# Input stage of a two-layer decoder: turning tokens, high and low parts and the first weight slots

## The reference

```python
def rms_norm(x, w):
    x32 = x.astype(jnp.float32)
    y = x32 * lax.rsqrt(jnp.mean(x32 * x32, axis=-1, keepdims=True) + NORM_EPS)
    return (y * w.astype(jnp.float32)).astype(x.dtype)

def swiglu(x, w_gate, w_up, w_down):
    return (jax.nn.silu(x @ w_gate) * (x @ w_up)) @ w_down
```

## Time and profile before

| | us |
|---|---|
| median of 3 runs | 2236.66 |
| lowest and highest | 2235.32 to 2239.92 |
| profiled execution, device time | 2238.05 |
| its span in the profile | 2236.3 |
| TensorE busy in it | 2173.0 (97%) |
| VectorE busy | 1013.6 (45%) |
| ScalarE busy | 760.5 (34%) |

### The profile page before, as it was taken

The page is one execution under the profiler, slowest core; times in us unless marked ns, Lnnn a source line. Parts: engine busy times, 40 slices in busy tenths (PEclk is TensorE's granted clock), DMA queues, the critical chain, the costliest instruction groups (busy, mean ns, idle before and its releaser), DMA issues.

```text
span 2236.3 us, 38348 instructions
## 1 busy us (share of the span) xinstructions
PE 2173.0 (97%) x16050; PEld 2050.6 (92%) x16050; DVE 1013.6 (45%) x1385; ACT 760.5 (34%) x1232; POOL 111.1 (5%) x105
## 2 busy tenths in 40 slices
PE   6999999999989899999999999999999999999998
PEld 5999999998989889999999999999998788888887
DVE  5544422666475364444216444421663346444423
ACT  3322222335433443222224322222352454222222
POOL 2000000100032100000000000000000010000000
PEclk9999999999899999999999999999999999999999
DMA  3333332321110113323321333332232122333232
GB/s 100 104 93 87 98 117 81 74 77 43 44 39 1 46 50 104 94 85 104 104 84 48 103 94 92 97 104 75 64 86 67 47 58 84 94 94 94 93 113 76
DMA packets 328447, 179.69 MB, mean 80 GB/s; under 512 B 15834, under 2 KB 323329, under 8 KB 328351
## 3 DMA queue, kind: packets, MB, share of 16 engines
q1 hardware_dynamic: 326992, 175.30, 27.0%
q0 software_dynamic: 1024, 2.86, 0.5%
q10 hardware_dynamic: 334, 0.14, 0.0%
HBM read 176.16 MB, written 2.12 MB: 80 GB/s over the span
## 4 chain that ended last, share of the span: by engine, by line
PE 93%; DVE 3%; ACT 2%; DMA 1%; issue 1%; POOL 0%; ACTq 0%; DVEq 0%; POOLq 0%
PE psum L591 67%; PE psum L603 10%; PE psum L791 5%; PE psum L2226 1%; DVE w_hl L514 1%; PE psum L1781 1%; PE psum L2243 1%; PE psum L2693 0%; PE psum L1756 0%; PE psum L657 0%; DMA rows_vec<-dn_norm_w 0%; PE psum L2709 0%; PE psum L2704 0%; DMA stage<-even_w_in 0%; PE psum L1741 0%
## 5 line engine op out<-in xcount | busy, mean ns | idle before, releaser
L591 PE MATMUL psum<-x_hl,w_hl 128*128 128x264 f32 (+1 forms) x9120 | 1242.9, 299 | 9.3 <-DVE w_hl L514 3.8
L591 PEld LDWEIGHTS psum<-x_hl,w_hl 128*128 128x128 f32 x9120 | 1187.4, 190 | 60.7 <-issue 12.1
L514 DVE TENSOR_TENSOR w_hl<-stage,w_hl 128x1024 fp32r<-128x1024 f32 (+1 forms) x310 | 396.0, 1277 | 366.3 <-ACT w_hl L507 366.2
L507 ACT ACTIVATE w_hl<-stage 128x1024 fp32r<-128x1024 f32 (+1 forms) x310 | 339.8, 1097 | 234.3 <-PE psum L591 92.1
L591 PE MATMUL psum<-acts,w_hl 128*128 128x264 f32 x2376 | 288.9, 284 | 0.0
L591 PEld LDWEIGHTS psum<-acts,w_hl 128*128 128x128 f32 x2376 | 288.6, 188 | 0.0
L1332 DVE TENSOR_TENSOR t_both<-psum,rinv 128x528 f32<-128x528 f32 (+1 forms) x88 | 61.9, 703 | 303.4 <-PE psum L591 303.4
L1134 ACT ACTIVATE acts<-t_both 128x528 f32 (+3 forms) x88 | 56.6, 643 | 399.5 <-DVE t_both L1335 399.5
L603 PE MATMUL psum<-x_hl,w_hl 128*128 128x264 f32 (+1 forms) x1344 | 175.6, 290 | 6.8 <-DVE w_hl L514 4.6
L603 PEld LDWEIGHTS psum<-x_hl,w_hl 128*128 128x128 f32 x1344 | 169.6, 193 | 10.1 <-DVE w_hl L514 5.0
L1326 DVE TENSOR_TENSOR t_both<-psum,rinv 128x528 f32<-128x528 f32 (+1 forms) x88 | 61.9, 703 | 182.6 <-PE psum L591 182.5
(11 more groups left out here) (325 smaller groups left out, 1322.2 us busy)
## 6 DMA issues: line engine op xcount, KB each, us to landing
stage<-ffn_w_gate SPq DMA_DIRECT2D x88, 512.0 KB, 3.8
stage<-ffn_w_up SPq DMA_DIRECT2D x88, 512.0 KB, 3.8
stage<-ffn_w_down SPq DMA_DIRECT2D x48, 704.0 KB, 4.7
stage<-odd_w_in SPq DMA_DIRECT2D x24, 512.0 KB, 3.9
stage<-ffn_w_down SPq DMA_DIRECT2D x22, 512.0 KB, 3.4
stage<-even_w_in SPq DMA_DIRECT2D x18, 512.0 KB, 4.2
stage<-even_w_out SPq DMA_DIRECT2D x8, 512.0 KB, 3.7
stage<-odd_w_out SPq DMA_DIRECT2D x8, 512.0 KB, 3.6
```

The costliest lines, as they stand in the source:

```text
L507: act.activation(weights(core.w_hl[:, slot.ring, 0, :], *kind), weights(core.stage[:, slot.stage, :], *kind), ACT.Copy).then_inc(core.w_hi, 1)
L514: dve.tensor_tensor(weights(core.w_hl[:, slot.ring, 1, :], *kind), weights(core.stage[:, slot.stage, :], *kind), weights(core.w_hl[:, slot ...
L591: op = pe.matmul(out, lhs, moving[:, moved, kt, t0:t0 + n], start=first and part + moved == 0, stop=last and part == 1)
```

## The change

The tokens load as two transfers, features 0 to 511 first, the others behind the first slot's weights. TensorE waits only for identity and norm weights, turns these, then turns k-tiles 0 and 1 and from then on runs products of the first two slots between the turns: slot 0's k-tile two before the turned one behind each turn from the third on, and two k-tiles of slot 1 behind each of the last three turns. The other constants come after the last turn. Two double banks take turns for the turned k-tiles. ScalarE makes the high parts straight from PSUM, a left side of 272 tokens and a right side of 256, while VectorE copies the other side into `h`; then VectorE makes the low part, ScalarE the square into a buffer of its own for each k-tile. The weight splits of slots 0, 1 and 2 stand at k-tiles 0, 3 and 5. After all eight, VectorE adds the squares of four, two and one k-tiles in three additions in place of GpSimd's eight operations. The token sum moves two k-tiles ahead of the end of slot 2. The core of the diff (left out: constants of the counting in `Norm.count`, semaphores, unused ones removed):

```diff
 ROW_BANKS = (5, 7, 4, 6)
+INPUT_SIDES = ((0, META + 2 * P, 0), (META + 2 * P, 2 * P, 1))
+INPUT_SLOTS = 2
...
+        self.in_squares = self.at("in_squares", [P, DT, TOK], self.arena + 4 * FT * TOK)
...
 def sync_program(core, sp, a):
-    sp.dma_start(core.rows_x, a["x"][0].rearrange("(b p) d -> p b d", p=P)).then_inc(core.tok_in, 16)
+    load_tokens(core, sp, a, 0)
     sp.dma_start(core.rows_meta[:, :], a["meta_tokens"]).then_inc(core.tok_in, 16)
...
+def load_tokens(core, sp, a, half):
+    cols = slice(half * D // 2, (half + 1) * D // 2)
+    sp.dma_start(core.rows_x[:, :, cols], a["x"][0].rearrange("(b p) d -> p b d", p=P)[:, :, cols])\
+        .then_inc(core.tok_right if half else core.tok_in, 16)
+
+
 def load_slot(core, sp, a, phase, i, u):
     slot = Slot(phase, i, u)
+    if phase is core.phases[0] and slot.peeled and slot.local == 1:
+        load_tokens(core, sp, a, 1)
     if not slot.peeled or slot.count() > 2:
         sp.wait_ge(core.w_lo, slot.count(2))
...
+def input_bank(kt):
+
+    return 4 + 2 * (kt % 2)
+
+
+def tensor_input(core, pe, phase):
+
+
+    k = core
+    slots = [Slot(phase, 0, u) for u in range(INPUT_SLOTS)]
+
+    def turn(kt):
+        if kt >= 2:
+            pe.wait_ge(k.x_hi, kt - 1)
+            pe.wait_ge(k.h_new, 2 * (kt - 1))
+        if kt == 0:
+            pe.wait_ge(k.tok_in, 32)
+        elif kt == DT // 2:
+            pe.wait_ge(k.tok_right, 16)
+        cols = slice(kt * P, (kt + 1) * P)
+        bank = input_bank(kt)
+        pe.transpose(k.psum[:, bank, 0:META], k.rows_meta[0:META, cols], k.ident[0:META, 0:META])
+        for b in range(NBLK):
+            at = META + b * P if b < 2 else (b - 2) * P
+            op = pe.transpose(k.psum[:, bank + b // 2, at:at + P], k.rows_x[:, b, cols], k.ident[:])
+        op.then_inc(k.tok_flip, 1)
+
+    def run(slot, kt):
+        if kt == 0:
+            pe.wait_ge(k.w_lo, slot.count())
+        pe.wait_ge(k.x_lo, kt + 1)
+        slot.out_pair = slot.pair
+        op = products(k, pe, phase, slot, kt, kt, k.x_hl, kt == 0, kt == DT - 1)
+        if kt == DT - 1:
+            op.then_inc(k.slot_used, 1)
+
+    turn(0)
+    turn(1)
+    pe.wait_ge(k.cols_ready, 1)
+    for kt in range(2, DT // 2 + 1):
+        turn(kt)
+        run(slots[0], kt - 2)
+    for kt in range(DT // 2 + 1, DT):
+        turn(kt)
+        run(slots[0], kt - 2)
+        run(slots[1], 2 * (kt - DT // 2 - 1))
+        run(slots[1], 2 * (kt - DT // 2 - 1) + 1)
+    pe.wait_ge(k.x_hi, DT)
+    pe.wait_ge(k.h_new, 2 * DT)
+    pe.wait_ge(k.consts_set, 5)
+    pe.wait_ge(k.consts_in, 16 * (CONST_LOADS - SCALAR_LOADS))
+    pe.wait_ge(k.vectors_in, 16 * (SCALAR_LOADS - 2))
+    pe.transpose(k.psum[:, 7, 2 * P:2 * P + VEC_ROWS], k.rows_vec[0:VEC_ROWS, :], k.ident[0:VEC_ROWS, 0:VEC_ROWS])
+    pe.matmul(k.psum[0:QH, 6, 0:512], k.table[:], k.bucket_hot[:, 0:512], start=True, stop=True)
+    pe.matmul(k.psum[0:QH, 7, 0:V_ALL - 512], k.table[:], k.bucket_hot[:, 512:V_ALL], start=True,
+              stop=True).then_inc(k.cols_flip, 1)
+    for slot in slots:
+        run(slot, DT - 2)
+        run(slot, DT - 1)
+
...
+        tensor_input(k, pe, phase)
+    elif not whole_first:
         tensor_first(k, pe, phase)
+    done = INPUT_SLOTS if begins else RING - 1 if whole_first else RING
     for slot in group:
         weights_ready(slot)
...
-                token_sum(k, pe, phase.before)
             op = products(k, pe, phase, slot, kt, kt, k.x_hl, kt == 0, kt == DT - 1)
             if kt == DT - 1:
                 op.then_inc(k.slot_used, 1)
 
     def step(i, u):
-        if isinstance(i, int) and i == 0 and (u < RING - 1 or not whole_first):
+        if isinstance(i, int) and i == 0 and u < done:
             return
         slot = Slot(phase, i, u)
         slot.out_pair = slot.pair
@@ -902,8 +980,9 @@
         weights_ready(slot)
         if turned:
             pass
-        elif phase.kind != "out" and isinstance(i, int) and i == 0:
-            pe.wait_ge(k.root_ready, 1)
+        elif begins and isinstance(i, int) and i == 0:
+            if u == RING - 1:
+                pe.wait_ge(k.root_ready, 1)
         elif phase.kind == "out" and slot.local == RING - 1:
             pe.wait_ge(k.even.o_full, NBLK + 1)
         elif not (isinstance(i, int) and i == 0):
@@ -917,6 +996,8 @@
             else:
                 pe.wait_ge(k.scaled, i * RING + (u + phase.evac0 - RING + 1))
         for kt in range(DT):
+            if begins and isinstance(i, int) and i == 0 and u == INPUT_SLOTS and kt == DT - 2:
+                token_sum(k, pe, phase.before)
...
 def token_sum(core, pe, norm):
 
-    pe.wait_ge(core.sq_added, DT)
+    pe.wait_ge(core.sq_added, 3)
+    pe.wait_ge(core.cols_ready, 4)
...
 def tensor_program(core, pe):
     k = core
-    pe.wait_ge(k.consts_set, 5)
-
-    pe.wait_ge(k.vectors_in, 16 * SCALAR_LOADS)
-    pe.wait_ge(k.consts_in, 16 * (CONST_LOADS - SCALAR_LOADS))
...
-    for kt in range(DT):
-        pair = (kt + 2) % RING
-        if kt >= 2:
-            pe.wait_ge(k.h_new, max(kt - RING + 1, 1))
-            pe.wait_ge(k.cols_ready, 4)
-        pe.transpose(k.psum[:, 2 * pair, 0:META], k.rows_meta[0:META, kt * P:(kt + 1) * P], k.ident[0:META, 0:META])
-        for b in range(NBLK):
-            at = META + b * P if b < 2 else (b - 2) * P
-            op = pe.transpose(k.psum[:, 2 * pair + b // 2, at:at + P], k.rows_x[:, b, kt * P:(kt + 1) * P], k.ident[:])
-        op.then_inc(k.tok_flip, 1)
-    pe.wait_ge(k.h_new, DT)
+    pe.wait_ge(k.norms_in, 32)
+    pe.transpose(k.psum[:, 0, 0:12 * DT], k.rows_norm[0:12 * DT, :], k.ident[0:12 * DT, 0:12 * DT])\
+      .then_inc(k.cols_flip, 1)
     for kind, step in k.steps:
         if kind == "dense":
             tensor_dense(k, pe, step)
...
+def scalar_input(core, act):
+
+
+    k = core
+    first = k.phases[0]
+    act.wait_ge(k.cols_flip, 1)
+    act.activation(k.norm_cols[:, :], k.psum[:, 0, 0:12 * DT], ACT.Copy).then_inc(k.cols_ready, 1)
+    act.wait_ge(k.cols_ready, 1)
+
+    def square(kt):
+        act.wait_ge(k.h_new, 2 * kt + 2)
+        act.activation(k.in_squares[:, kt, :], k.h[:, kt, :], ACT.Square).then_inc(k.sq_made, 1)
+
+    for kt in range(DT):
+        col = first.before.pre_col + kt
+        for side, (t0, n, bank) in enumerate(INPUT_SIDES):
+            if side == 0:
+                act.wait_ge(k.tok_flip, kt + 1)
+            else:
+                act.wait_ge(k.h_new, 2 * kt + 1)
+            act.activation(k.x_hl[:, 0, kt, t0:t0 + n], k.psum[:, input_bank(kt) + bank, 0:n], ACT.Copy,
+                           scale=k.norm_cols[:, col:col + 1]).then_inc(k.x_hi if side else k.in_high, 1)
+        if kt:
+            square(kt - 1)
+        if kt in INPUT_SPLITS:
+            split_hi(k, act, Slot(first, 0, INPUT_SPLITS.index(kt)), (DT, P))
+    square(DT - 1)
+    act.wait_ge(k.cols_flip, 2)
+    act.activation(k.vec_cols[:, 0:VEC_ROWS], k.psum[:, 7, 2 * P:2 * P + VEC_ROWS], ACT.Copy).then_inc(k.cols_ready, 1)
+    act.activation(k.bias_row[0:QH, 0:512], k.psum[0:QH, 6, 0:512], ACT.Copy).then_inc(k.cols_ready, 1)
+    act.activation(k.bias_row[0:QH, 512:V_ALL], k.psum[0:QH, 7, 0:V_ALL - 512], ACT.Copy).then_inc(k.cols_ready, 1)
+
+
 def scalar_norm(core, act, norm):
     k = core
     if norm.split:
         scalar_split(k, act, norm)
         return
     load_table(k, act, ACT.Sqrt)
-    for kt in range(DT):
-        act.wait_ge(k.h_new, norm.h0 + kt + 1)
-        tile = k.h[:, kt, norm.t0:TOK]
-        col = norm.pre_col + kt
-        act.activation(k.x_hl[:, 0, kt, norm.t0:TOK], tile, ACT.Copy,
-                       scale=k.norm_cols[:, col:col + 1]).then_inc(k.x_hi, 1)
-        if kt >= 2:
-            act.wait_ge(k.sq_added, kt - 1)
-        buf = k.t_up if kt % 2 else k.t_gate
-        act.activation(buf[:, norm.t0:TOK], tile, ACT.Square).then_inc(k.sq_made, 1)
-        if kt == DT // 2:
-            split_ahead(k, act, split_hi, norm.next, 0, 0)
+    split_ahead(k, act, split_hi, norm.next, 0, 0)
     root(k, act, norm)
     load_table(k, act, ACT.Silu)
+    act.wait_ge(k.bias_stored, 16)
 
 
...
 def scalar_program(core, act, a):
     k = core
-    for dst, src in const_rows(k, a)[0:SCALAR_LOADS]:
+    for dst, src in const_rows(k, a)[0:2]:
+        act.dma_start(dst, src).then_inc(k.norms_in, 16)
+    for dst, src in const_rows(k, a)[2:SCALAR_LOADS]:
         act.dma_start(dst, src).then_inc(k.vectors_in, 16)
-    split_hi(k, act, Slot(k.phases[0], 0, 0), (DT, P))
-    act.wait_ge(k.cols_flip, 1)
-    act.activation(k.norm_cols[:, :], k.psum[:, 0, 0:12 * DT], ACT.Copy).then_inc(k.cols_ready, 1)
-    act.activation(k.vec_cols[:, 0:VEC_ROWS], k.psum[:, 1, 0:VEC_ROWS], ACT.Copy).then_inc(k.cols_ready, 1)
-    act.activation(k.bias_row[0:QH, 0:512], k.psum[0:QH, 2, 0:512], ACT.Copy).then_inc(k.cols_ready, 1)
-    act.activation(k.bias_row[0:QH, 512:V_ALL], k.psum[0:QH, 3, 0:V_ALL - 512], ACT.Copy).then_inc(k.cols_ready, 1)
-    act.wait_ge(k.consts_set, 5)
```

(78 more changed lines are left out.)

6 lines of the change are left out of this document (removed).

## The result

The changed kernel takes **2224.03 us** (median of 5, 2222.86 to 2225.03) against 2236.66: ratio 0.9941, 95% interval 0.9929 to 0.9953. The profiled execution took 2223.76, its span 2222.0.

A forecast was written before the change was run, and what follows sets the result against it. TensorE is busy for 97% of the span, so only the start, before products run, can pay. The fourth slot starts at 42.9 instead of 50.26, a gain of 7.4 us: 2236.66 becomes 2229.3, range 2226 to 2234.5.

The forecast's parts named there:

- The rise of TensorE's clock: At the start, among turns and products: TensorE stays at the low level until 26.3 us, then runs at the high one.
- the fourth slot: End of the start: the fourth weight slot's products begin at 42.9 us instead of 50.26, a gain of 7.4 us.
- everything after it should move with it: Behind the fourth slot's start: all later work shifts by the same time, so that start alone judges the change.
- an uncertainty of 1 or 2: Whole time: the shown runs lie 4.6 us apart, which adds 1 or 2 us of uncertainty to the range.
- no new gap: Sign to look for: TensorE shows no new gap behind the fourth slot.
- The rule weighed: Turns among products: transposes don't raise the clock, so they would hold it down and the gain would be gone.
- rivals 1 and 3: Clock stays low through last turn and constants (2237.0, milder 2234.0; chance 0.14 together), or through slot 2 (2243.7; 0.04).
- Rival 4: Start: clock rises at once with the first units, VectorE's pace sets the end; fourth slot 40.8, time 2227.2, chance 0.15.
- The first turn: Start of TensorE's transposes: at 10.0 us, an estimate between the bounds 8 and 13.4.
- Packets, low parts, pace: Loads and k-tiles at the start: 2 KB packet 0.085 us, low part 0.755, k-tiles 1.75 apart, longer across splits.
- rival 2: Token load: 2 KB packets cost 0.16 us, so halves gain nothing; fourth slot 46.3, time 2232.7, chance 0.12.
- Squares, root, later splits: VectorE before and behind the fourth slot: additions take 4.5 us from 31.5; these, root and fifth slot's split stay hidden.

The follow-up runs named there:

- turns_first: The changed kernel with all eight turns ahead of all products: median 2230.67 us, ratio 0.997.
- before_pad2: The kernel before with twelve more products, computed twice, ahead of the fourth slot: median 2236.61 us, ratio 0.9993.
- whole_load: The changed kernel with the tokens loaded as one transfer again: median 2230.07 us, ratio 0.9956.
- after_pad1: The changed kernel with six more products, computed twice, ahead of the fourth slot: median 2225.27 us, ratio 0.994.
- after_pad2: The changed kernel with twelve more products, computed twice, ahead of the fourth slot: median 2229.13 us, ratio 0.9951.
- gpsimd_adds: The changed kernel with GpSimd adding the eight squares one by one again, VectorE's three additions gone: median 2223.93 us, ratio 0.9927.
- before_early: The kernel before with the early start alone (tokens in halves, identity and norm rows waited for alone, other constants behind the turns): median 2234.05 us, ratio 0.9981.

## Why the prediction was wrong, point by point

- **The rise of TensorE's clock is the term that failed at the fourth slot.** The step read "the level rose 3.4 us after the first product before, so I take the high level from 26.3", for it counted only units that ran unbroken. It rose at 18.7, 4.4 us after the first product, with a whole turn in between. The work that the forecast had done at 26.3 was done at 23.06: 3.24 earlier, 0.24 of it from the start (first products at 14.31, not 14.55), **3.0 from the clock**. Later terms gave 0.6 back: the two blocks of a turn and three units 2.93 and 2.92 instead of 2.7, constants 1.53 instead of 1.4, 60 products 7.46 instead of 7.3, together 0.7, of which 0.14 was already in the forecast's roundings. The miss at the fourth slot is 2.65; by the seven traces with the changed start it is 2.2.
- **That alone would have left the time in the range.** 2229.3 less 2.65 is 2226.65, above the lower end of 2226. The other 2.6 come from "everything after it should move with it", which put any difference of low time in the later stages at nothing, or at "an uncertainty of 1 or 2". Means of all executions say what was there: 2238.2 - 2224.3 = 13.9, of which 2208.4 - 2197.4 = 11.0 is left without the low time, near the 10.3 gained at the slot. The other **2.9 are half of the 5.8 us** by which the changed kernel spent less time at the low level behind the first rise (53.9 against 59.7, standard errors 0.9 and 0.5). So everything after it did move with it, and "no new gap" holds; the low time did not stay the same. Why it is shorter is **open**: it follows neither the start of the fourth slot nor the added products in order (55.1 and 56.5 with products added before, 54.3 to 58.6 with products added to the changed kernel). The baseline hid part of the miss: the median of three, 2236.66, lies 1.5 below the mean of the 69 executions.
- **The rule weighed.** The Trainium skill, TensorE: Matmul & The Clock Gate, Part 4 (PE-mode transpose), says that the clock does not go up for transposes. Transposes alone stayed at 1.04 for four up to 24.13 in turns_first, as it says, and so to their end in four more of the six traces that turn before all products. In the sixth, before_pad2, the level rose in the last turn, with no product yet run but the constants' four, which had ended 8.7 us before; TensorE had worked for 11.8 us without a pause. Its last two turns' transposes of tokens:

```profile
23.21 1.11 PE L963 MATMUL psum<-ident,rows_x 128*128 128x128 f32 x4
...
24.42 0.66 PE L963 MATMUL psum<-ident,rows_x 128*128 128x128 f32 x4
```

  So the rule does not hold without exception here. Nor did turns hold the clock down between products in any of the twelve traces that have them there: rivals 1 and 3 did not come.
- **Rival 4 had the nearest number (40.8), and half of its mechanism.** The clock did not rise at once, and in this trace TensorE had no wait from 14.31 on. But the pace of ScalarE and VectorE stood only 0.05 us behind it (28.86 against 28.91), so an earlier rise would have gained next to nothing: the other traces that rose early have the same 25.9 from first products to fourth slot (whole_load, after 3.4 us; after_pad1, 3.8; after_pad2, 4.4).
- **The first turn** came at 8.17 instead of 10.0, within its bounds. It gained nothing, since products wait for the first weights, landed at 11.92 (forecast 12).
- **Packets, low parts, pace:** 2 KB packet 0.085 as taken, so rival 2 is out; low part 0.77 (0.755); k-tiles 1.65 apart (1.75), 3.6 across the splits at 3 and 5 (3.7). Across the split at 0 it was 4.45 and not about 3: the first low part came early, over at 11.45 for the forecast's 13.2, and then the split waited for the weights. That cost nothing.
- **Squares, root, later splits:** the additions took 4.4 (4.5), 1.55 earlier than forecast (29.95 for 31.5), and were hidden, as were root and fifth slot's split. gpsimd_adds shows that leaving them on GpSimd would have cost 0.85 us at most at the fourth slot.
- **What the parts are worth at the fourth slot:** products between turns 6.35 (turns_first), loading in halves 3.7 (whole_load), squares about 0.85 at most. The early start without the new order 2.4 of the 10.0 (before_early). Each is one trace against one, with the spread of some 2 us told above. They overlap and are no sum.

## What to carry to other kernels

Put products between the transposes as soon as both can run: they fill the time in which the transposes wait for other engines to empty their banks (4.1 us in turns_first), and the level rose early enough that the later turns took half (1.05 to 0.59 for four). An early start was worth little here as long as one engine's queue had a late load's work ahead of the early work; look at the order on each queue first. When later stages mix narrow and wide matmuls, time a gain of a few microseconds in several executions, and read their mean granted clock beside the times: here half of the low time explains what the start does not.

## What the hardware showed that was not expected

- The rate rises although transposes stand between the products: 4.4 us after the first product in the changed kernel, with one turn in between, and 3.8 to 6.4 in the seven traces with its start. By the excess over 0.1215 a product, against 0.222 at the low level, it rises some 3.1 us after it in turns_first and 4.7 in before_early, both unbroken, and 3.4 to 6.3 in the kernel before and its padded form (138 products in 18.32 and in 19.60). So it is not one constant distance.
- One and the same stretch of a mixer takes 110.1 or 113.7 us in executions of one kernel, and the rest behind the fourth slot 2059.7 to 2065.2; over 18 traces each microsecond at the low level adds 0.52 to the rest.
- The level can rise in transposes alone: once in six traces (before_pad2, at about 24.2 us).
- GpSimd's small packets are dear for the others: 37 packets of its queue held 48.7% of 16 engines for a microsecond, 0.21 us each on average. They are of several kinds in the trace: 18 of 4 bytes took 0.01 each, 8 of 128 bytes and 7 of 256 bytes 0.32 and 0.58. The 11 of ScalarE's queue are 6 of 4 bytes and 5 of 512 bytes, 0.025 on average. Delaying GpSimd's gave 1.5 us at the fourth slot, 1.8 by the means of three and seven traces. The Trainium skill, DMA: Bandwidth & Descriptors, Specifications, asks for 512 B or more in a transfer for the full rate; the trace agrees, though here size and queue change together, and no run parts them.
- VectorE beside GpSimd: a low part takes 0.77 alone, 0.87 beside a spread addition and 1.83 beside additions without a pause.
